# Stick-breaking attention: running totals from a high and a low part, and two gates that share one change of function

## The reference, cut to what matters

```
z = q @ k.T * scale                      # queries t, keys s
log_1m = where(s < t, log_sigmoid(-z), 0)
after = reverse running total of log_1m over the keys, without the key itself
w = where(s < t, exp(log_sigmoid(z) + after), 0)
out = w @ v
```

## Time and profile before

| | |
|---|---|
| median of 3 runs | 955.1 us (953.59 to 955.68) |
| the profiled execution's own time | 957.95 us |
| its span in the profile | 956.2 us |
| mean granted clock of TensorE | 0.994 of 2.4 GHz |
| PE busy | 934.0 us, 98% |
| DVE busy | 640.4 us, 67% |
| ACT busy | 522.2 us, 55% |

### The profile page before, as it was taken

How to read it: one execution, slowest core, us unless ns; L and a number is a source line. 1 busy time by engine, 2 the same in 40 slices (tenths; PEclk the granted TensorE clock), 3 DMA queues, 4 the chain that set the end, 5 groups by cost and what they waited for, 6 DMA issues and landing times.

```text
span 956.2 us, 19525 instructions
## 1 busy us (share of the span) xinstructions
PE 934.0 (98%) x8649; PEld 903.9 (95%) x8649; DVE 640.4 (67%) x737; ACT 522.2 (55%) x613; POOL 2.1 (0%) x14
## 2 busy tenths in 40 slices
PE   8899999999999999999999999999999999999998
PEld 7899999999999999999899998999889999999998
DVE  2897887865586455667689876465666665466565
ACT  3545444445555568954585663377556654454445
POOL 0000000000000000000000000000000000000000
PEclk9999999999999999999999999999999999999998
DMA  9999557874568444467354444143326466555521
GB/s 339 355 361 340 176 168 233 288 240 141 168 220 262 136 133 133 130 211 234 98 172 134 136 131 134 51 128 132 110 66 212 134 208 223 185 177 192 176 97 45
DMA packets 153439, 172.30 MB, mean 180 GB/s; under 512 B 4000, under 2 KB 137692, under 8 KB 153228
## 3 DMA queue, kind: packets, MB, share of 16 engines
q1 hardware_dynamic: 151696, 167.43, 54.1%
q10 hardware_dynamic: 1660, 3.63, 1.1%
HBM read 170.00 MB, written 1.05 MB: 179 GB/s over the span
## 4 chain that ended last, share of the span: by engine, by line
PE 50%; DVE 5%; ACT 3%; issue 1%; DVEq 0%
PE pj L2588 39%; PE pj L2547 1%; PE pj L2549 1%; PE pj L2548 1%; ACT w_hi L931 1%; PE pj L2403 1%; PE m_all L2042 1%; PE m_all L2310 1%; PE m_all L2293 1%; PE m_all L2437 1%; PE m_all L2464 0%; DVE w_lo L1432 0%; DVE work L1859 0%; PE m_all L2296 0%; DVE small L1860 0%
## 5 line engine op out<-in xcount | busy, mean ns | idle before, releaser
L1432 DVE TENSOR_TENSOR w_lo<-raw,w_hi 128x2048 fp32r<-128x2048 f32 (+1 forms) x126 | 285.3, 2269 | 133.0 <-ACT w_hi L931 132.3
L2588 PE MATMUL pj<-h_hi,w_hi 128*128 128x256 f32 x1224 | 348.1, 284 | 3.4 <-DVE h_lo L1868 1.1
L2588 PE MATMUL pj<-h_lo,w_hi 128*128 128x256 f32 x1224 | 342.0, 279 | 0.0
L2588 PE MATMUL pj<-h_hi,w_lo 128*128 128x256 f32 x1224 | 341.7, 279 | 0.0
L931 ACT ACTIVATE w_hi<-raw 128x2048 fp32r<-128x2048 f32 (+1 forms) x126 | 237.8, 1890 | 52.7 <-PE pj L2588 34.5
L2588 PEld LDWEIGHTS pj<-h_hi,w_hi 128*128 128x128 f32 x1224 | 229.2, 187 | 8.4 <-issue 6.1
L2588 PEld LDWEIGHTS pj<-h_lo,w_hi 128*128 128x128 f32 x1224 | 229.4, 187 | 0.4
L2588 PEld LDWEIGHTS pj<-h_hi,w_lo 128*128 128x128 f32 x1224 | 229.2, 187 | 0.2
L2588 PE MATMUL pj<-y_hi,w_hi 128*128 128x256 f32 x592 | 166.1, 281 | 1.0 <-issue 0.8
L2588 PE MATMUL pj<-y_lo,w_hi 128*128 128x256 f32 x592 | 165.3, 279 | 0.0
L2588 PE MATMUL pj<-y_hi,w_lo 128*128 128x256 f32 x592 | 165.1, 279 | 0.0
(11 more groups left out here) (404 smaller groups left out, 1106.8 us busy)
## 6 DMA issues: line engine op xcount, KB each, us to landing
raw<-in_odd_in_w_dram SPq DMA_DIRECT2D x28, 1024.0 KB, 5.5
raw<-in_w_in_dram SPq DMA_DIRECT2D x23, 1024.0 KB, 5.4
raw<-in_ada_w_dram SPq DMA_DIRECT2D x22, 1024.0 KB, 7.1
raw<-in_w_ff_in_dram SPq DMA_DIRECT2D x16, 1024.0 KB, 5.3
raw<-in_w_ff_out_dram SPq DMA_DIRECT2D x16, 1024.0 KB, 5.3
raw<-in_even_in_w_dram SPq DMA_DIRECT2D x13, 1024.0 KB, 5.1
raw<-in_even_out_w_dram SPq DMA_DIRECT2D x8, 1024.0 KB, 5.7
raw<-in_odd_out_w_dram SPq DMA_DIRECT2D x8, 1024.0 KB, 5.7
```

What stands on the lines that cost most here:

```text
L1432: V.tensor_tensor(lo[:, 0:n], raw_of(u)[:, 0:n], hi[:, 0:n].bitcast(F32), ALU.subtract).then_inc(done, 1)
L2588: m = nc.tensor.matmul(to, a_, b_, start=(s == 0 and q == 0 and (fb == 0 or not together)), stop=(s == len(steps_) - 1 and q == 2), skip_g ...
```

## The change

Three things are done.

1. `sb_z` on DVE: behind the mask, log_1m (`sbw(2)`) is copied to `sb_hi` as fp32r (a tensor_copy) and the rest, `sbw(2) - sb_hi`, is written to `sb_lo` as fp32r. Each waits for the one before it through `link`. `sb_l` is signalled by the last. Ahead of head 0, two constants are copied once as fp32r.
2. `sb_c` on PE: the two float32 matmuls become four fp32r matmuls, both constants for `sb_hi` and for `sb_lo`.
3. The gate jobs 0 to 4 are projected only; their evacuations stand later. Behind slot 1 of `left`, `open_gate` applies silu to gga 0 and gga 1, and then asks once for the set with exp and ln. The rest of gga 0 and gga 1 stands behind slot 2, gga 2 behind slot 3, gga 3 and ggb 0 behind slot 4. The other three gates are as before.

```diff
     left = list(sbs)
-    log_exp_next = [(name, i) for name in ("gga", "ggb") for i in range(4)][:len(left)]
-    for i in range(8):
-        odd("gga" if i < 4 else "ggb", "gate", 5136 if i < 4 else 6160, i % 4)
-        for st in left[i] if i < len(left) else []:
-            step(*st)
-        if i >= 4:
-            schedule.append(("ada_out", gate_units[i - 4]))
-    assert len(left) <= 8
+    opened = [("gga", 0), ("gga", 1)]
+    gate_jobs = [("gga", i) for i in range(4)] + [("ggb", i) for i in range(4)]
+    finished_behind = {2: gate_jobs[0:2], 3: gate_jobs[2:3], 4: gate_jobs[3:5]}
+    for n, (name, i) in enumerate(gate_jobs):
+        odd(name, "gate", 5136 if name == "gga" else 6160, i)
+        if n < len(left):
+            early(name, i)
+            for st in left[n]:
+                step(*st)
+        if n == 1:
+            for key in opened:
+                step("open_gate", key)
+        for key in finished_behind.get(n, ()):
+            finish(*key)
+        if n >= 4:
+            schedule.append(("ada_out", gate_units[n - 4]))
+    assert len(left) == 5
...
+        sb_const = tuple(work_r[:, 55, a:a + P] for a in (0, P))
+        sb_hi, sb_lo = (work_r[:, 52:56, :].rearrange("p c t -> p (c t)")[:, a:a + 384] for a in (0, 384))
...
+            def open_gate(key):
+                g = gates.index(key)
+                projected(act, key)
+                if g >= 2:
+                    act.wait_ge(S("y_f"), g - 1)
+                done_reading(nc.scalar.activation(gate_tmp("sg", g), bank_of(key)[:, :], ACT.Silu if jobs[key]["kind"] == "gate" else ACT.Relu), key)
+                if key == opened[-1]:
+                    act.preload_act_table_set(LOG_EXP)
...
-                    projected(act, key)
-                    if g >= 2:
-                        act.wait_ge(S("y_f"), g - 1)
-                    done_reading(nc.scalar.activation(gate_tmp("sg", g), two, ACT.Silu if kind == "gate" else ACT.Relu), key)
-                    if key in log_exp_next:
-                        act.preload_act_table_set(LOG_EXP)
+                    if key not in opened:
+                        open_gate(key)
                     act.wait_ge(S("y_f"), g + 1)
...
             def sb_z(h):
+                if h == 0:
+                    for to, name in zip(sb_const, ("from_here", "ones")):
+                        link(V.tensor_copy(to, K(name)))
...
                 link(V.scalar_tensor_tensor(out=sbw(2), in0=sbw(0), scalar=0.0, in1=sbw(1), op0=ALU.max, op1=ALU.add))
-                V.tensor_tensor(sbw(2), sbw(2), K("sb_mask"), ALU.mult).then_inc(S("sb_l"), 1)
+                link(V.tensor_tensor(sbw(2), sbw(2), K("sb_mask"), ALU.mult))
+                link(V.tensor_copy(sb_hi, sbw(2)))
+                V.tensor_tensor(sb_lo, sbw(2), sb_hi.bitcast(F32), ALU.subtract).then_inc(S("sb_l"), 1)
...
-                nc.tensor.matmul(M[1][:, 0:384], K("from_here"), sbw(2), start=True, stop=False, skip_group_check=True)
-                nc.tensor.matmul(M[1][:, P:2 * P], K("ones"), sbw(2)[:, 2 * P:3 * P], start=False, stop=True, skip_group_check=True).then_inc(S("sb_c_done"), 1)
+                from_here, ones = sb_const
+                for part in (sb_hi, sb_lo):
+                    nc.tensor.matmul(M[1][:, 0:384], from_here, part, start=(part is sb_hi), stop=False, skip_group_check=True)
+                    m = nc.tensor.matmul(M[1][:, P:2 * P], ones, part[:, 2 * P:3 * P], start=False, stop=(part is sb_lo), skip_group_check=True)
+                m.then_inc(S("sb_c_done"), 1)
```

More of the change, by code:

```diff
@@ L649, in program @@
             "p (c t) -> p c t", c=8) for c in (E_["lev1"], E_["lev2"])]
-        gates = [k for kind, k in schedule if kind == "job" and jobs[k]["kind"] in ("gate", "relu2")]
+        gates = [k for kind, k in schedule if kind in ("job", "evacuate") and jobs[k]["kind"] in ("gate", "relu2")]
         def x_tok(q):
@@ L1281, in _ @@
                          turn_p=turn_p, split_p=split_p, ple_x=ple_x, ple_post=ple_post, load_x=load_x, first_sum=first_sum, params=params, modulate=modulate, first_split=first_split, second_split=second_split, norm_part=norm_part, norm=norm, final_part=final_part, sgu_v=sgu_v, windows=windows, gla_z=gla_z, gla_decay=gla_decay, gla_kt=gla_kt, gla_o=gla_o, gla_n=gla_n, sb_z=sb_z, sb_c=sb_c, sb_o=sb_o)
+            def open_gate(key):
[6 more added lines that the diff above has]
+                    act.preload_act_table_set(LOG_EXP)
+            steps["open_gate"] = open_gate
             def evac(key):
```

## The result

The changed kernel takes 960.41 us (median of 4 runs, 960.08 to 962.41) against 954.62 us before (4 runs, 953.59 to 955.68). The ratio is 1.0069, 95% interval 1.0057 to 1.0082: 5.4 to 7.8 us slower. The forecast was 960.0 us in a range of 957.2 to 962.8, with 86% on slower.

What follows compares the result with a forecast made beforehand. PE bounds the kernel, waiting on ACT and DVE around the heads; after the change those two set the pace. One chain's final lateness, +4.9 us (its late points not added), on the median 955.1 gives 960.0 us, range 957.2 to 962.8.

Steps and rivals of the forecast that it cites:

- What bounds the stretch: Heads stretch: PE leads today, waiting 1.69 us for log_1m; after the change DVE and ACT set the pace.
- Part 1: Running totals on PE: 0.57 us per head instead of 0.87, saving 2.4 us of PE's work that buys nothing.
- Part 2: High and low part on DVE: a copy of about 0.35 us and a subtraction make `sb_l` 1.0 us later.
- the loop: Round between DVE and ACT per head, argument to next argument: 6.90 us before, 7.9 after, against PE's slot of 7.45.
- Part 3: Moved gates: eight loads (10.3 us) saved on ACT, but queue order makes the last gate job 4.9 to 5.0 us late.
- The waits: PE's new waits: about 0.9 us at heads 4 to 6, 3.3 and 2.8 at head 7, 0.4 and 1.8 for w_lo.
- The prediction's books: Cross-check on PE: new waits of 9.2 us less 4.1 us of saved work and old waits give 5.1 us.
- Faster: Rival: ACT's relief reaches PE, head 6's argument starting before about 382; -4.1 us, 951.0 us; 7%.
- slower still: Rival: the copy costs 0.60 us with the link (+6.4 us, 961.5), or PE loses clock; 961 to 964 us; 16%.
- The drain: Possible 1380 ns per change of set on ACT; three on the chain would end it some 4 us later; not counted.
- No change: Rival: finished gates' round trips overlap better, only the first late point (0.3 us) is left; 955 to 957 us; 7%.
- the totals do not get cheaper: Rival: totals take 1.74 us, PE's slot 8.6 us, longer than DVE and ACT's round; 962 to 964 us; 4%.

Runs made afterwards that it cites:

- PE kept busy: The changed kernel plus six float32 matmuls with overwritten sums, issued in PE's wait ahead of head 7's totals: ratio 1.0058 to the kernel before.
- copies early: The changed kernel with its two copies of constants moved from head 0's step to the first gla_n step on DVE: 960.14 us, ratio 1.0052 to the kernel before.
- the gates alone: The kernel before with the gates moved as in the change, the running totals left in float32: ratio 1.0038 to the kernel before.
- the totals alone: The kernel before with totals from a high and a low part, the gates left where they were with their own loads: ratio 1.0038 to the kernel before.

## Why the prediction was right, point by point

**What bounds the stretch.** Right. PE's old waits are gone, its saved work doesn't show, and the pace is set by DVE and ACT.

**Part 1.** 0.57 us of totals per head were forecast, between 0.48 and 0.6. With PE at full clock, from the first of the four matmuls to the next product, head 0 has 0.52 us (334.46 to 334.98) and heads 1 to 6 have 0.60 to 0.63 (380.83 to 381.46 for head 6). It dropped out of the sum, as said.

**Part 2.** The copy takes 0.36 us (forecast 0.35) and `sb_l` comes 0.99 us later. The ln of heads 5 and 6 are 7.87 us apart (370.22 and 378.09, forecast 7.9). One term was put at nothing and was not: the two copies of the constants "lie in DVE's wait for the first ln". They do end long before it, at 328.2. But the first maximum starts 0.99 us after the first ln and not 0.56 us, as it did before, and the loop carries these 0.43 us to the end: the first round took 8.31 us (330.44 to 338.75). Moving the copies brought back 0.45 us, which is the size of the difference between the forecast of 4.9 and the 5.37 us of the stretch. The cause stays open. One thing can be said: DVE's idle time ahead of this maximum is 3.22 to 3.26 us in all fourteen profiles, with the copies and without them, as if it counted from DVE's last instruction and not from the ln; the copies put the end of that instruction 0.40 us later.

**Part 3.** The chain from head 6's ln to the last gate job holds at every step to within 0.3 us. Counted from the first mark (subtract 0.62 us from the forecast's times): head 6's ln forecast 377.9, measured 378.09; head 7's totals forecast 391.5, measured 391.76; `sb_o` of head 7 forecast 400.6, measured 400.76; the last gate job forecast 415.4, measured 415.63. The waits of 0.4 and 1.8 us for w_lo came out as 0.39 and 1.55.

**The waits.** 3.3 us at head 7's totals was 3.12. At `sb_o` 2.8 us was forecast and 1.09 measured, because the clock fell and the job between took longer: from 392.88 to the start of the wait 6.8 instead of 5.6 us. The prediction had put that inside the wait, and with PE kept busy the wait was 2.56 and the stretch the same. The three small waits forecast at heads 4 to 6 (0.9 us in all) stand in no bracket of the timeline, but they show in the starts: from the last product with v to the totals it is 0.14 us at head 1, 0.43 at head 3 and 0.49 to 0.50 at heads 4 to 6. That makes 1.4 us, and it begins one head earlier. The prediction's books close with these, as an estimate: 6.15 us of waits in brackets, 1.4 of small ones and about 1.7 of slower clock, less 1.7 of old waits and 2.1 of cheaper totals, are some 5.4 us.

**The rivals.** *Faster* hung on whether the split stands ahead of the argument, and the run that moves the argument shows both sides of it: with the split ahead 5.4 us slower, behind it 2.3 to 3 us faster. Of *slower still*, the two-source price of the copy is out (0.36 us), and the clock did fall, inside the next wait. *The drain* of 1380 ns with each change of set (the Trainium skill, ScalarE: Activation LUTs, What ACT_TABLE_LOAD costs) does not show after the change either: load at 378.63, silu at 379.92, 1.29 us. *No change* and *the totals do not get cheaper* are out by the rows above.

**The size.** The stretch gives 5.4 us, the medians 5.8 and the ratio 6.6 (5.4 to 7.8). The two kernels that should take nearly the same time gave 5.5 (PE kept busy) and 5.0 us (copies early, where 0.45 less was due). So about 5.4 us is the best estimate of what the change costs, half a microsecond more than the forecast's 4.9. That the time itself, 960.41 us, comes within 0.4 us of the forecast's 960.0 is in part luck: the forecast started from a median of three runs of the kernel before, 955.1 us, and with the fourth it is 954.62.

## What to carry to other kernels

When helper engines take strict queues, write down for each queue what stands in front of the instruction that the other engine waits for; a relief of 10 us on a busy engine is worth nothing, or less, if it pulls apart work that used to overlap. Moving one short instruction ahead of a long one that waits for another engine was worth 8 us here, and cost 1.6 us in the kernel before, where the split had hardly waited (0.25 us) and ran beside ACT's loads of a set. After each such gain ask what is late next, past the end of the stretch one is looking at.

## What was not expected of the hardware

- At head 0, with PE at full clock and straight behind the matmuls of a job, the high part's 384 columns start at 334.46, its 128 at 334.63, the low part's 384 at 334.69, its 128 at 334.92, and the next product at 334.98. So in fp32r the 384 columns take 0.17 us the first time and 0.23 the second, and 128 columns 0.06 us, the lower of the prediction's two bounds. All four take 0.52 us there; at heads 1 to 6, straight behind a product with v, the first 384 columns take 0.25 to 0.29 us and all four 0.60 to 0.63. The two in float32 take 0.87.
- The first maximum of the eight heads starts 0.97 to 1.00 us after its ln in the nine profiles that have two unrelated copies right ahead of its wait, and 0.55 or 0.56 us in the five that don't, among them the one that has the copies 32 us earlier. The cause is open.
- The length of one wait doesn't decide whether the granted clock falls behind it. It fell behind waits of PE of 3.12 us (0.62 from 392 to 396 us), 2.86, 2.56 and 1.95 us (0.57 in four microseconds each). It stayed at 1.00 behind 1.09 us (400 to 404 us after the change), behind 2.27 us with the gates alone, and behind 2.11, 2.12 and 2.10 us with the totals alone.
